# One block from attention to the last norm, output projection begun in the sample phase's drain, and ScalarE weighting one pair of heads

## What is computed

```python
h = rms_norm(x, norm_mix_pre)
# one projection feeds four GLA heads and eight NSA heads
gla_q, gla_k, gla_v, gla_g, gr, nsa_q, nsa_kv, nsa_g = project(h, ...)
y_gla = gla_output(gla_chunked(...))               # linear attention
# NSA: softmax attention in three branches, mixed by sigmoid gates
o = g[0] * o_cmp + g[1] * o_slc + g[2] * o_win     # p of each branch / its sum, times its gate
y = concatenate([y_gla, y_nsa], axis=-1) @ w_out   # output projection, 1024 x 1024
x = x + rms_norm(y, norm_mix_post)
h = rms_norm(x, norm_ffn_pre)
u = square(relu(h @ w_ff_up))                      # 1024 x 4096
return x + rms_norm(u @ w_ff_down, norm_ffn_post)  # 4096 x 1024
```

## Time and profile before

| | us |
|---|---|
| median of three runs (lowest, highest) | 2010.68 (2005.02, 2014.06) |
| the profiled execution: time | 2013.24 |
| the same: span from first to last instruction | 2011.5 |

### The profile page before, as it was taken

The page is one execution under the profiler, slowest core; times in us unless marked ns, Lnnn a source line. Parts: engine busy times, 40 slices in busy tenths (PEclk is TensorE's granted clock), DMA queues, the critical chain, the costliest instruction groups (busy, mean ns, idle before and its releaser), DMA issues. The chain is left out here.

```text
span 2011.5 us, 26094 instructions
## 1 busy us (share of the span) xinstructions
PE 1904.3 (95%) x10662; PEld 1545.7 (77%) x10662; DVE 676.9 (34%) x1546; ACT 524.1 (26%) x1178; POOL 547.7 (27%) x458
## 2 busy tenths in 40 slices
PE   7999999979999699999979979999999999999997
PEld 5888887745555477777758868888888888888885
DVE  5321213567665333334221054300332133123313
ACT  3311212377677434334320060000100000000002
POOL 3222222147665211111103152222222222222224
PEclk9999999879999799999979989999999999999998
DMA  4011222130000575656504011111111111111112
GB/s 134 22 47 49 75 51 64 43 109 1 1 1 1 183 260 182 223 179 232 165 16 143 22 43 42 43 42 42 42 42 42 43 43 42 42 42 43 42 53 84
DMA packets 113630, 149.73 MB, mean 74 GB/s; under 512 B 21584, under 2 KB 99320, under 8 KB 105256
## 3 DMA queue, kind: packets, MB, share of 16 engines
q1 hardware_dynamic: 104296, 80.95, 13.4%
q0 software_dynamic: 9216, 67.11, 9.9%
HBM read 139.96 MB, written 12.27 MB: 76 GB/s over the span
## 5 line engine op out<-in xcount | busy, mean ns | idle before, releaser
L278 PE MATMUL PS<-Z,ring 128*128 128x258 f32 x1152 | 258.2, 380 | 0.0
L1830 PE MATMUL PS<-Z 128*128 128x256 f32 (+1 forms) x1024 | 244.8, 386 | 0.0
L278 PEld LDWEIGHTS PS<-Z,ring 128*128 128x128 f32 x1152 | 218.1, 189 | 33.0
L278 PE MATMUL PS<-hT,ring 128*128 128x258 f32 x992 | 226.8, 386 | 7.8 <-DMA ring<-in_w_out 7.2
L1830 PEld LDWEIGHTS PS<-Z 128*128 128x128 f32 x1024 | 186.6, 190 | 42.8 <-issue 20.3
L278 PEld LDWEIGHTS PS<-hT,ring 128*128 128x128 f32 x992 | 190.4, 193 | 37.8 <-DMA ring<-in_w_out 7.3
L2376 ACT ACTIVATE Z<-PS 128x516 f32<-128x516 f32 x80 | 48.2, 602 | 641.3 <-PE PS L278 641.3
L241 POOL TENSOR_TENSOR Z<-ring 128x512 f32<-128x512 f32 x36 | 46.9, 1303 | 599.7 <-PE PS L278 533.4
L278 PE MATMUL PS<-Z 128*128 128x258 f32 x832 | 187.1, 380 | 0.0
L278 PEld LDWEIGHTS PS<-Z 128*128 128x128 f32 x832 | 157.5, 189 | 23.9
L2396 DVE TENSOR_TENSOR Z<-PS,Z 128x516 f32<-128x516 f32 x96 | 66.8, 696 | 314.9 <-PE PS L278 314.9
(11 more groups left out here) (381 smaller groups left out, 2717.5 us busy)
## 6 DMA issues: line engine op xcount, KB each, us to landing
ring<-in_w_ff_up SPq DMA_DIRECT2D x32, 512.0 KB, 5.3
ring<-in_w_ff_down SPq DMA_DIRECT2D x32, 512.0 KB, 4.4
ring<-in_w_in SPq DMA_DIRECT2D x9, 1024.0 KB, 5.1
X<-in_x_prompt SPq DMA_DIRECT2D x8, 1024.0 KB, 11.2
srow<-in_state_nsa_win SPq DMA_DIRECT2D x16, 256.0 KB, 5.3
out_y_prompt<-X SPq DMA_DIRECT2D x8, 512.0 KB
out_win_sample<-in_state_nsa_win SPq DMA_DIRECT2D x1, 4088.0 KB
out_kv_prompt<-Z SPq DMA_DIRECT2D x8, 256.0 KB, 2.0
```

Source lines behind the costliest of these rows:

```text
L278: last = nc.tensor.matmul(M.PS[:, bank_of(M, n, e) + c, 0:CW], a[:, k, :], b[:, k, c * CW:(c + 1) * CW], start=e in (M1, M2, M5) and k == ...
L1830: last = nc.tensor.matmul(out, w1s[:, v, half, 2 * r + e, :], x2[seg][:, r, v, :, e, half:half + SEG[seg]], start=(j == 0), stop=(j == 15))
```

## The change

1. `phase_attend` to the last `phase_norms` stand in one block. The meetings between them (five) are gone, and waits on semaphores at the data take their place.
2. `phase_sample` begins the output projection. At tau 137 to 144 TensorE issues, one piece per tau and ahead of that tau's tail step, the products M1 and M2 of the first pair, each piece two matmuls (4 records). SyncE loads the weights of the first two pairs after the values of pair 2, GpSimd makes the first pair's sums after its last gather, and VectorE makes t1 to t4 after its last tail step: all columns but the last 8 at once, the last 8 after `store`.
3. `weighted`: the selected branch of key head 1 goes to ScalarE in every unit, not only in those of query tiles 0 to 2.

The diff, without changes of indentation alone and cut to its core:

```diff
 def bank_of(M, n, e):
+    if e == M2 and n == 0 and M.dense.ahead:
+        return 4
 def seven_products(...):
+        if n == 0 and e in st.ahead:
+            continue
 def phase_norms(nc, M, A, O, block, use, front, back):      # its own nc.Block() is gone
             elif back is not None:
                 for s in range(2):
+                    dense.wait_product(sp, KD // 2 - 2 + s, M4)
             def turn_front(t):
+                if t == 0:
+                    for e in (M4, M3):
+                        dense.wait_moved(pe, len(dense.kinds) - 1, e)
 def phase_attend(nc, M, A, O, block):
-                if (kvh == 1 and (br != SEL or SU[n][0] <= 2)) == on_scalar]
+                if (kvh == 1) == on_scalar]
 def phase_sample(nc, M, A, O, block):      # gpsimd, after the gathers
+            pool.wait_ge(xt, NG * B - 1)
+            pool.wait_ge(vcp, NG * B - 1)
+            pool.wait_ge(kt, NG * B - 1)
+            X.st.wait_loaded(pool, 0)
+            weight_sums(nc, pool, X.st, pair_slot(M, 0), 0)
         # sync, before and after its loads
+            sp.wait_ge(S("pv_group"), M.all_groups)
+            sp.wait_ge(tpe, on_pe(2, PV))
+            for n in range(2):
+                mix_weights(sp, M, A, n)
+            sp.wait_ge(tact, on_act(NPAIR - 1, YV))
+            mix_loads(sp, M, A)
         # tensor
+            def output_piece(i):
+                e, h, b = (M1, 0, X.h11) if i < 4 else (M2, 1, X.h21)
+                if i == 0:
+                    X.st.wait_loaded(pe, 0)
+                    pe.wait_ge(gel, 4 * B)
+                    pe.wait_ge(sev, B)
+                k = i % 4
+                for c in range(2):
+                    last = nc.tensor.matmul(M.PS[:, bank_of(M, 0, e) + c, 0:CW], pair_slot(M, 0)[:, KQ * h + k, 0:P],
+                                            b[:, k, c * CW:(c + 1) * CW], start=(k == 0), stop=(k == KQ - 1),
+                                            skip_group_check=True)
-            pe.wait_ge(ready, 1)
+            pe.wait_ge(S("y_moved"), M.all_units)
                 if 0 <= b < B:
                     conv_piece(b, i)
+                if 0 <= tau - CONV - 16 * B < 8:
+                    output_piece(tau - CONV - 16 * B)
         # vector, before and after its steps
+            dve.wait_ge(S("pv_group"), M.all_groups)
+            nc.vector.tensor_tensor(X.t1, X.h12, X.h11, ALU.subtract).then_inc(X.hsum, 1)
+            dve.wait_ge(X.hsum, 1)
+            dve.wait_ge(conv, 4 * B)
+            dve.wait_ge(kt, NG * B)
+            dve.wait_ge(vcp, NG * B)
+            mix_sums(nc, dve, M, slice(0, HN - B))
+            dve.wait_ge(tact, on_act(NPAIR - 1, YV))
+            mix_sums(nc, dve, M, slice(HN - B, HN))
+def mix_sums(nc, dve, M, c):
+    nc.vector.tensor_tensor(X.t2[:, :, c], X.h22[:, :, c], X.t1[:, :, c], ALU.subtract).then_inc(X.hsum, 1)
+    dve.wait_ge(X.hsum, count)
+    nc.vector.tensor_tensor(X.t3[:, :, c], X.t2[:, :, c], X.h11[:, :, c], ALU.subtract).then_inc(X.hsum, 1)
+    nc.vector.tensor_tensor(X.t4[:, :, c], X.h21[:, :, c], X.t2[:, :, c], ALU.subtract).then_inc(X.hsum, 1)
 def phase_mix_out(nc, M, A, block_):
-                        pe.wait_ge(hsum, {M6: 2, M5: 2, M7: 3, M4: 4}[e])
+                        pe.wait_ge(hsum, {M6: 5, M5: 1, M7: 6, M4: 7}[e])
 def phase_ffn(nc, M, A, O, block_):
+            pe.wait_ge(M.sem("hT_written"), 2 * (QT + 1))
+            dve.wait_ge(M.sem("hT_written"), 2 * (QT + 1))
+            dve.wait_ge(M.sem("y_stored"), 16)
```

More of the change, by code:

```diff
@@ new lines, in _, with reduce @@
+    @block.vector
+    def _(dve):
+        ch = Chain(dve, step)
+        def reduce(n, i):
+            qt, gp, j0, ls, lw = shape(n)
+            g, c = i // nchunk[n], i % nchunk[n]
+            m, cc = 2 * n + g, first_chunk[n] + i
+            offs = (RSEL + RWIN + (T - P) // CSTR - qt * P // CSTR, T - P - qt * P, RSEL + (j0 - qt) * P + WIN)
+            dve.wait_ge(scores, cc + 1)
+            if i == 0 and n >= 3:
+                dve.wait_ge(turned, first_group[n - 2])
+            for kvh in range(KVH):
@@ L1699, in _ @@
[L1699 to L1713 removed]
+                    p0 = (CMP0, SEL0, WIN0)[br] + k0
@@ new lines, in _ @@
+        pe.wait_ge(S("y_moved"), M.all_units)
+        for tau in range(LAST):
+            b, i = divmod(tau - CONV, 16)
+            if 0 <= b < B:
+                conv_piece(b, i)
+            if 0 <= tau - CONV - 16 * B < 8:
+                output_piece(tau - CONV - 16 * B)
+            if group(tau) is not None:
+                turn(*group(tau))
+            for off, what in ((8, lambda b: scores(b, 0)), (16, lambda b: scores(b, 1)), (13, window_keys),
+                              (15, window_scores), (22, compressed_keys), (23, compressed_scores),
+                              (26, compressed_values)):
+                if sequences(tau, off) is not None:
+                    what(sequences(tau, off))
+            for off, what in ((10, new_scores), (25, group_sum), (27, spread_mask), (28, turn_compressed),
+                              (28, turn_maxima), (29, turn_back), (30, sums), (32, turn_probs), (33, turn_probs_window),
+                              (34, values), (37, outputs)):
+                if pairs(tau, off) is not None:
+                    what(pairs(tau, off))
@@ new lines, in _ @@
+    @block_.scalar
+    def _(act):
+        for n in range(NP):
+            for e in st.on_act(n):
+                st.wait_product(act, n, e)
+                nc.scalar.activation(halves(place(*tiles(n), e)), bank_view(M, n, e), ACT.Copy).then_inc(st.act, 1)
+    @block_.vector
+    def _(dve):
+        for n in range(NP):
+            for e in ADDED:
+                out = place(*tiles(n), e)
+                st.wait_product(dve, n, e)
+                st.wait_moved(dve, n, {M2: M1, M7: M5, M3: M6}[e])
+                nc.vector.tensor_tensor(halves(out), bank_view(M, n, e), halves(out), ALU.add).then_inc(st.dve, 1)
@@ L2420 @@
+            st.wait_moved(dve, n, M4)
+            nc.vector.tensor_tensor(u21[:, k, :], u21[:, k, :], u21[:, k, :], ALU.mult).then_inc(step, 1)
+            dve.wait_ge(step, made(up_pairs, SQ21))
+            nc.vector.tensor_tensor(ut4[:, k, :], u21[:, k, :], ut2[:, k, :], ALU.subtract).then_inc(step, 1)
+            up_pairs += 1
 OUTS = [
```

1693 lines of the change are left out of this document (825 added, 868 removed).

## The result

The changed kernel takes 1988.16 us (median of 4 runs, 1987.05 to 1990.07) against 2010.73: a ratio of 0.9884, 95% interval 0.9868 to 0.99, so 22.6 us. Its profiled execution took 1987.59 us, the span is 1985.7: 25.8 less than the span of before.

| stage | before | after | gain | forecast |
|---|---|---|---|---|
| up to attention's first score | 397.7 | 398.0 | -0.3 | 0 |
| prompt attention, first score to last product | 272.3 | 260.6 | 11.7 | 5.0 |
| from there to the first convolution | 19.8 | 16.1 | 3.7 | 5.3 |
| first to last convolution | 335.2 | 335.6 | -0.4 | 0 |
| last convolution to M5 of the output projection | 47.2 | 33.2 | 14.0 | 13.4 |

A forecast was written before the change was run, and what follows sets the result against it. TensorE, busy 95% of the span, was taken as the bound, with gains only from its pauses and half-clock stretches. 5.0 + 5.3 + 13.4 + 0.8 = 24.5 us gave 1986.2 us against the median 2010.68; 8-in-10 range 1976 to 1999.

The forecast's parts named there:

- part 1: Prompt attention: twenty weighting pieces moved from GpSimd to ScalarE shorten pauses at unit starts; +5.0 us (2 to 8).
- part 3: Output projection begun in the drain, so little stands between `store` and M6; +13.4 us (5 to 17).
- part 2: Start of the sample phase: without the meeting, gathered groups are worked on as they land; +5.3 us (3.5 to 7).
- pauses gone: Prompt attention: clock gain added for long pauses that vanish at unit starts; 0.8 us.
- The other estimate: Start of the sample phase: SyncE's earlier loads would hold up the first gather, making the gain 3.9 us.
- The joint: From `store`'s end to M6: 16.6 us shrink to 0.75 for ScalarE's copy and two hand-overs; +15.9 us.
- The chain: Drain: the added pieces lengthen its dependent steps, partly offset by a clock back for the values; -1.5 us.
- R1: Rival: the clock is held in the drain, part 3 is 16.8 us, time 1982.8; 18%.
- The cover: Behind the drain: VectorE's four sums, 9.3 us, become last if the drain shortens by more than 6 us.
- Part 4: The other meetings, before the second norm, feed-forward phase and last norm, are gone; +0.8 us (0.3 to 1).
- R4: Rival: ScalarE becomes the pace of prompt attention, which is 26 us longer; time 2028; 4%.
- R3: Rival: gathers land together and ScalarE ends last at unit starts in GpSimd's place; time 1994.0; 8%.

The follow-up runs named there:

- e2: Changed kernel with the weighting of before (GpSimd again has the selected branch of units with more than three query tiles): 1996.1 us, ratio 0.9923.
- e1: Kernel before with the weighting change alone: 1999.7 us, ratio 0.9946.
- e5: Changed kernel with one meeting of all engines put back between prompt attention and the sample phase: 1995.8 us, ratio 0.9919.
- e4: Changed kernel with SyncE's first window loads held until VectorE has transposed the third gathered group: 1988.0 us, ratio 0.9887.
- e3: Changed kernel without the eight pieces in the drain, M1 and M2 computed behind it: 1993.1 us, ratio 0.9907.
- e6: Changed kernel with three meetings put back, ahead of second norm, feed-forward phase and last norm: 1986.8 us, ratio 0.9877.
- e12: e7's gathers, last norm's own block and M5 started ahead of M6, plus ScalarE taking another window branch in units 1, 2, 14, 15: 1984.7 us, ratio 0.9865.
- e7: Changed kernel with the sample phase's first three gathers issued one by one behind GpSimd's last three weightings: 1985.5 us, ratio 0.9868.

## Why the prediction was right, and where it wasn't

The time (1988.2 for 1986.2 forecast) came out as the sum of steps that were off in both directions: by the profiles part 1 gave 6.7 us more than forecast and part 3 0.6 more, part 2 gave 1.6 less, and 3.3 were lost in a place that was in no step. The mechanisms of parts 2 and 3 were right; that the sum came this near is in part luck.

**Part 1: the term that was mis-sized is the clock.** The pauses went as forecast at units 3, 5 and 6, less at unit 2 (1.0 for 1.5) and unit 4 (0.15 for 0.7). At units 2, 3 and 4 ScalarE's weighting is now the last (it ends at 438.92, 457.01 and 473.71, TensorE starts 0.1 later), which is why units 2 and 4 gained less, and which the prediction had named as a sign that the step fails; it holds for these starts, not for the sum. Unit 9 got a pause of 0.71 in the same way. For "pauses gone" the sum added 0.8, with the price of a fall read from eight turns (0.9). The windows show 1.7 for each fall, since the lower clock lasts beyond the turns. Two falls are gone (3.5 us) in every kernel with the changed weighting; one of them stood behind the 1.43 at unit 4, where the prediction saw eight turns at the upper clock and read no fall. And 2.6 of the trace's 11.7 is scatter. By the medians the edit gives 8.0 in e2 and 10.9 in e1, at and above the high end of 8.

**Part 2: the meeting's worth was right.** With the meeting put back (e5) and an attention of the same length this joint is 5.6 longer; in e2, with the weighting of before, the first convolution comes 14.7 us after attention's end instead of 19.8: 5.1 for 5.3 forecast. The changed kernel's trace shows 3.7, because attention's end, which the prediction held fixed against the gathers' issue, came a microsecond nearer to it, and the wait for the first gather took that back. No run shows that part 1 did this: kernels with the same weighting have it both ways, and e1 has 4.5 us, as before. The other estimate, 3.9, came from the Trainium skill's page "DMA: Bandwidth & Descriptors" (section Queues, rings and completion order), by which each DMA engine takes turns between the queues. It is near 3.7 by chance: e4 shows that the first gather isn't held up by SyncE's loads (6.04 against 6.14 us), only the fourth (5.93 against 6.73).

**Part 3: right in sum, with two errors that cancel.** The joint gave 15.7 for 15.9. The chain gave +1.1 for -1.5: the clock was held throughout, which was R1's case (+0.9), and e3 shows that the pieces hold it. The +5.0 that R1 needs was more than its rows give (twice 1.7 for the values and 0.9 for `turn_probs`, 4.2), and 2.3 of the chain's gain came in e3 without any piece. M6 cost 2.9 for 1.0, more than the 2.6 of the low end. R1's reasoning on the drain was the better one; its time failed at M6. The cover held: the last of VectorE's four long sums ended at 1032.9, 3.3 us ahead of `store`'s end, where the prediction had put more than 6, so the next shortening has to look there.

**Part 4: 0.5 for 0.8, and a loss of 3.3 beside it.** A meeting behind which nothing had to be waited for was worth 0.25, 0 and 0.25 by the traces before and after; the three put back cost 0.4 together in e6. That joining blocks could lengthen the end of the last one was in no rival.

**R4** didn't occur, but it was nearer than its one start in five: with the changed weighting a pause ends on ScalarE at units 2, 3, 4, 9 and 11, five of the ten. e12 shows its mechanism with 3 to 4.3 us for eight moved pieces. ScalarE's 194 of 272 us, the argument against R3, stands in a window of the trace of before and not in the table that the prediction names.

## What to carry to other kernels

Price a pause by the granted clock of the whole stretch behind it, not by the first instructions: here a fall cost 1.7 us or more on top of its pause, behind some pauses and not behind others of the same length, and 1.3 us of pause ahead of M6 made M6 2.9 us longer. When the stretch ahead of a joint can end earlier, work out who is last there then: here an attention that ended earlier only waited longer for a gather whose issue had not moved, and moving the issue (e7) brought the first convolution 2 to 3.6 us nearer. Before you move work to the engine with more room, look for starts where it ends close to last: its whole queue counts there, not its busy share. Compare the ends of both engines; the bracket of a row names only one of them.

## What the runs showed of the hardware

- A meeting that came after GpSimd's indirect gathers ended only when they had landed: in e5 the last one was issued at 658.4 and landed at 667.6, the engines were idle from 659.7, and the meeting ended at 668.05 (e1: landed 666.7, ended 667.15). Other meetings cost 0 to 0.3 us.
- The same instructions gave an attention of 260.6 or of 263 to 264 us, by where the clock fell ahead of unit 3 and behind unit 13. The same pause of 1.35 us at unit 13 was followed by a granted clock of 1.00 in the changed kernel and of 0.83 over ten microseconds in e6.
- The end of a last block that held everything from attention or from the sample phase on lay 5.3 to 5.5 us behind the issue of the last store, that of a block with the last one or two phases 2.2, in all fourteen profiles. The cause is open.
